# The host lays the chunked weights out so that each 2 MB chunk is 16 KB in a row per partition

## The reference, cut to what matters

```python
sh1, sc1, gt1, sh2, sc2, gt2 = adaln(c, ada_w[l], ada_b[l])       # ada_w: 1024 x 6144
...
x_mix, _, _ = token_mixer(hx @ w_in[l], lbs[l], s_f, s_b, *mix_args)   # w_in: 1024 x 6144
...
mixed = jax.nn.sigmoid(g_a) * (y_a @ w_pa) + jax.nn.sigmoid(g_b) * (y_b @ w_pb)
return mixed @ w_o
...
mod_x = silu_c @ ada_w[layer] + ada_b[layer]                       # second block, two layers
lat = project_in(h, w_in)                                          # w_in: 1024 x 3616
...
def squared_relu_mlp(h, w1, w2):                                   # 1024 x 4096, 4096 x 1024
    return jnp.square(jax.nn.relu(h @ w1)) @ w2
```

## Time and profile before

| | |
|---|---|
| runs | 2148.82, 2149.39, 2142.51 us; median 2148.82 |
| span of the profiled execution | 2142.0 us |
| TensorE busy / weight load | 2005.6 us (94%) / 1431.7 us (67%) |
| DVE, ACT, POOL busy | 34%, 28%, 18% |
| DMA packets | 120207, 428.28 MB |
| mean granted TensorE clock | 0.964 of full speed |

### The profile page before, as it was taken

How to read it: one execution, slowest core, us unless ns; L and a number is a source line. 1 busy time by engine, 2 the same in 40 slices (tenths; PEclk the granted TensorE clock), 3 DMA queues, 4 the chain that set the end, 5 groups by cost and what they waited for, 6 DMA issues and landing times.

```text
span 2142.0 us, 27488 instructions
## 1 busy us (share of the span) xinstructions
PE 2005.6 (94%) x11518; PEld 1431.7 (67%) x11518; DVE 724.0 (34%) x1201; ACT 594.7 (28%) x921; POOL 385.9 (18%) x183
## 2 busy tenths in 40 slices
PE   7799989999999999998999798999999899889998
PEld 2567787775444444446887646777777678579998
DVE  1523154323222222226343614222222535533333
ACT  2413112022222222223113414222332311534443
POOL 2400000000000000005003012333343010414653
PEclk9899978989999999999999899999999999998999
DMA  9268914447999999982224003344334232413450
GB/s 358 96 244 295 369 51 160 160 158 305 425 428 419 426 421 427 423 358 105 100 79 150 1 30 138 138 143 171 137 137 140 78 106 94 157 52 145 158 187 29
DMA packets 120207, 428.28 MB, mean 200 GB/s; under 512 B 5690, under 2 KB 23141, under 8 KB 107456
## 3 DMA queue, kind: packets, MB, share of 16 engines
q1 hardware_dynamic: 118016, 416.56, 50.5%
q0 software_dynamic: 2112, 10.57, 1.4%
HBM read 426.07 MB, written 1.05 MB: 199 GB/s over the span
## 4 chain that ended last, share of the span: by engine, by line
PE 70%; PEld 5%; DVE 4%; issue 3%; ACT 3%; POOL 2%; PEldq 0%; DVEq 0%; ACTq 0%
PE bank L505 68%; PEld bank L505 5%; PE bank L520 1%; DVE H L1805 0%; DVE X L2344 0%; POOL arena L1723 0%; POOL arena L1722 0%; DVE arena L2288 0%; POOL arena L1727 0%; PEldq L494 0%; POOL arena L1725 0%; DVE H_low L1812 0%; POOL arena L1728 0%; DVE H L2260 0%; DVE ring_low L2158 0%
## 5 line engine op out<-in xcount | busy, mean ns | idle before, releaser
L505 PE MATMUL bank<-arena_r 128*128 128x512 f32 (+1 forms) x1920 | 560.7, 357 | 40.3 <-DVE H_low L1812 20.8
L505 PE MATMUL bank<-arena_r,ring_low 128*128 128x512 f32 (+2 forms) x1792 | 567.0, 349 | 20.5 <-DVE H_low L1812 17.5
L505 PEld LDWEIGHTS bank<-arena_r 128*128 128x128 f32 x1920 | 342.9, 192 | 138.9 <-issue 56.0
L505 PEld LDWEIGHTS bank<-arena_r,ring_low 128*128 128x128 f32 (+1 forms) x1792 | 333.5, 191 | 67.5 <-issue 21.8
L505 PE MATMUL bank<-arena 128*128 128x64 bf16 (+9 forms) x2684 | 329.3, 291 | 24.7 <-DMA arena<-in_hy_filt_w 11.9
L505 PEld LDWEIGHTS bank<-arena 128*128 128x128 bf16 (+4 forms) x2684 | 210.5, 141 | 128.1 <-issue 90.9
L505 PE MATMUL bank<-ring,arena 128*64 128x512 f32 x1024 | 278.2, 595 | 1.1 <-ACT arena L1423 0.7
L2344 DVE SCALAR_TENSOR_TENSOR X<-bank,mod,X 128x256 f32<-128x256 f32 x216 | 96.4, 481 | 394.0 <-PE bank L505 394.0
L505 PE MATMUL bank<-H_low,arena_r 128*128 128x512 f32 (+1 forms) x608 | 208.0, 342 | 0.0
L1749 POOL TENSOR_TENSOR ring_low<-ring,arena_r 128x2048 fp32r<-128x2048 f32 x32 | 146.6, 4603 | 118.5 <-ACT arena_r L1611 118.5
L1271 ACT ACTIVATE arena<-bank 128x512 f32<-128x512 f32 (+2 forms) x106 | 52.4, 496 | 413.5 <-PE bank L505 413.2
(11 more groups left out here) (263 smaller groups left out, 1908.0 us busy)
## 6 DMA issues: line engine op xcount, KB each, us to landing
ring<-in_moe_w_gate SPq DMA_DIRECT2D x32, 2048.0 KB, 13.7
ring<-in_w_mlp SPq DMA_DIRECT2D x32, 2048.0 KB, 8.3
ring<-in_w_in SPq DMA_DIRECT2D x26, 2048.0 KB, 8.8
ring<-in_ada_w SPq DMA_DIRECT2D x24, 2048.0 KB, 11.8
ring<-in_moe_w_up SPq DMA_DIRECT2D x17, 2048.0 KB, 9.2
H<-in_moe_w_down SPq DMA_DIRECT2D x16, 2048.0 KB, 16.1
arena<-in_moe_w_up SPq DMA_DIRECT2D x15, 2048.0 KB, 9.5
ring<-in_moe_w_down SPq DMA_DIRECT2D x15, 2048.0 KB, 16.3
```

Of the source, the lines that this page charges most:

```text
L505: ins = nc.tensor.matmul(o, l, r, start=start, stop=stop, skip_group_check=True)
```

## The change

The host cuts each of the matrices into the chunks that the kernel loads and writes every chunk as [128 partitions, k, n], so that the 16 KB of one partition follow each other. The kernel then loads a whole chunk as it stands. Sizes, order, semaphores, buffers and all compute instructions stay. For the chunks of 384 columns of `ada_w_2[1]` a partition has 12 KB in a row, for the 32 columns of the ranks 1 KB.

```diff
+def by_columns(w, n=512):
+    return np.ascontiguousarray(w.reshape(*w.shape[:-2], -1, P, w.shape[-1] // n, n).swapaxes(-4, -2))
+
+def by_rows(w, k=4):
+    return np.ascontiguousarray(w.reshape(*w.shape[:-2], -1, k, P, w.shape[-1]).swapaxes(-3, -2))
...
-        def cols(w, a, n):
-            return w[:, bass.ds(a, n)].rearrange("(k p) n -> p k n", p=P)
-
-        def rows(w, a, n):
-            return w[bass.ds(a, n), :].rearrange("(k p) n -> p k n", p=P)
-
...
-                load(n, cols(T["ada_w"], n * 512, 512), as_cols(n))
+                load(n, T["ada_w"][n], as_cols(n))
             for j in range(12):
                 n = win(j)
-                load(n, cols(T["w_in"], WIN_ORDER[j] * 512, 512), as_cols(n))
+                load(n, T["w_in"][WIN_ORDER[j]], as_cols(n))
...
-            load(MERGE, rows(T["w_proj_a"], 0, 512), as_rows(MERGE))
-            load(MERGE + 1, rows(T["w_proj_b"], 0, 512), as_rows(MERGE + 1))
+            load(MERGE, T["w_proj_a"], as_rows(MERGE))
+            load(MERGE + 1, T["w_proj_b"], as_rows(MERGE + 1))
...
-                    load(first + 2 * j, cols(T["w_in_2"][l], j * 512, 512), as_cols(first + 2 * j))
+                    load(first + 2 * j, T["w_in_2"][l][j], as_cols(first + 2 * j))
...
-                        load(n, cols(T["w_mlp1_2"][l], (i * 2 + h) * 512, 512), as_cols(n), i * per)
+                        load(n, T["w_mlp1_2"][l][i * 2 + h], as_cols(n), i * per)
...
-                        src = T["w_mlp2_2"][l].rearrange("(j k p) n -> j p k n", p=P, k=4)[i * 2 + h]
-                        load(n, src, as_rows(n), i * per)
+                        load(n, T["w_mlp2_2"][l][i * 2 + h], as_rows(n), i * per)
```

More of the change, by code:

```diff
@@ L281, in _ @@
             for n in range(RING):
-                load(n, cols(T["ada_w"], n * 512, 512), as_cols(n))
+                load(n, T["ada_w"][n], as_cols(n))
             for j in range(12):
                 n = win(j)
-                load(n, cols(T["w_in"], WIN_ORDER[j] * 512, 512), as_cols(n))
+                load(n, T["w_in"][WIN_ORDER[j]], as_cols(n))
                 for i in BEHIND[j] if j < 8 else [8 + j]:
                     n += 1
-                    src = cols(T["ada_w"], (4 + i) * 512, 512) if i < 8 else cols(T["ada_w_2"][0], (i - 8) * 512, 512)
+                    src = T["ada_w"][4 + i] if i < 8 else T["ada_w_2"][i - 8]
                     load(n, src, as_cols(n))
-            load(MERGE, rows(T["w_proj_a"], 0, 512), as_rows(MERGE))
-            load(MERGE + 1, rows(T["w_proj_b"], 0, 512), as_rows(MERGE + 1))
+            load(MERGE, T["w_proj_a"], as_rows(MERGE))
+            load(MERGE + 1, T["w_proj_b"], as_rows(MERGE + 1))
             for j in range(2):
                 n = MERGE + 2 + j
-                load(n, cols(T["w_out"], j * 512, 512), as_cols(n))
+                load(n, T["w_out"][j], as_cols(n))
             def expert(c, name, e, turns=None):
@@ L338, in _ @@
                 for j in range(7):
-                    load(first + 2 * j, cols(T["w_in_2"][l], j * 512, 512), as_cols(first + 2 * j))
-                load(first + 14, cols(T["w_in_2"][l], 7 * 512, 2 * RANK), as_cols(first + 14, 2 * RANK))
+                    load(first + 2 * j, T["w_in_2"][l][j], as_cols(first + 2 * j))
+                load(first + 14, T["w_rank_2"][l], as_cols(first + 14, 2 * RANK))
                 for j in range(2):
-                    load(first + 16 + j, cols(T["w_out_2"][l], j * 512, 512), as_cols(first + 16 + j))
+                    load(first + 16 + j, T["w_out_2"][l][j], as_cols(first + 16 + j))
                 with sp.Fori(0, 4) as i:
@@ L350, in _ @@
                             for a in range(2):
-                                load(n, cols(T["ada_w_2"][1], (i * 4 + h * 2 + a) * ADA_COLS, ADA_COLS), as_cols(n, ADA_COLS), i * per)
+                                load(n, T["ada_w_3"][i * 4 + h * 2 + a], as_cols(n, ADA_COLS), i * per)
                                 n += 1
-                        src = T["w_mlp2_2"][l].rearrange("(j k p) n -> j p k n", p=P, k=4)[i * 2 + h]
-                        load(n, src, as_rows(n), i * per)
+                        load(n, T["w_mlp2_2"][l][i * 2 + h], as_rows(n), i * per)
                         n += 1
@@ L2394 @@
         arrays[name] = np.ascontiguousarray(I[name][0].T)
-    for name in ("ada_w", "w_in", "w_proj_a", "w_proj_b", "w_out", "hy_filt_w1", "hy_filt_w2", "hy_filt_w3"):
+    for name in ("hy_filt_w1", "hy_filt_w2", "hy_filt_w3"):
         arrays[name] = I[name][0]
+    for name in ("ada_w", "w_in", "w_out"):
+        arrays[name] = by_columns(I[name][0])
+    for name in ("w_proj_a", "w_proj_b"):
+        arrays[name] = by_rows(I[name][0])[0]
     for name in ("moe_w_gate", "moe_w_up", "moe_w_down"):
@@ L2399 @@
         arrays[name] = a.reshape(NX, *a.shape[3:])
-    for name in ("ada_w_2", "w_in_2", "w_out_2", "w_mlp1_2", "w_mlp2_2"):
-        arrays[name] = I[name]
+    arrays["ada_w_2"] = by_columns(I["ada_w_2"][0])
+    arrays["ada_w_3"] = by_columns(I["ada_w_2"][1], 384)
+    arrays["w_in_2"] = by_columns(I["w_in_2"][:, :, 0:3584])
+    arrays["w_rank_2"] = by_columns(I["w_in_2"][:, :, 3584:], 2 * RANK)[:, 0]
+    arrays["w_out_2"] = by_columns(I["w_out_2"])
+    arrays["w_mlp1_2"] = by_columns(I["w_mlp1_2"])
+    arrays["w_mlp2_2"] = by_rows(I["w_mlp2_2"])
     arrays["wr"] = np.concatenate([I["moe_router_g_w"][0], I["moe_router_e_w"][0].transpose(1, 0, 2).reshape(D, NX)], axis=1)
```

## The result

The changed kernel is slower: 2159.72 us median of four runs (2155.59 to 2161.98) against 2148.43 us (2142.51 to 2149.39, four runs). The medians differ by 11.3 us. The ratio is 1.0061 (95% interval 1.0041 to 1.008), that is 13 us, with 9 to 17 us as its interval. The forecast was +8 us.

What follows compares the result with a forecast made beforehand. PE was taken to bound the kernel, with loads mattering only in the first 125 us. Start +10 us (16 less 6.0), then -2, gave +8 on the median: 2156.8 us, range 2139 to 2162.

Steps and rivals of the forecast that it cites:

- What bounds the kernel: Whole program: PE sets the pace; after some 130 us faster loads are hidden, so the first 125 us decide everything.
- Turns by piece: DMA engines alternate between q1 and POOL's queue by piece, whatever its size; a q1 turn costs POOL's loads 0.62 us, not 0.09.
- The filter tables: POOL's first loads, which PE's first matmul needs: 20 turns beside q1 bring them at 21 us instead of 11.89.
- `ctx`: The input POOL loads after `x` and `pos`: lands at 39.5 us, 14.5 us later, held up by q1's 16 KB pieces.
- The sum beside POOL: DVE's two-operand sum at line 1857, held by up to one POOL split instruction: 0 to 3.4 us, taken as 1.5.
- D: Delay of PE's sums of squares in the start: 16 us, bounds 13 and 18.5; it also moves the end of `spectrum(1)`.
- The gift of 6.0 us: DVE's `norm` runs free ahead of POOL's second split, leaving 11 instructions instead of 26: 6.0 us less.
- After the start: Chunk 9 landing earlier, -1.0 us, and PE's own load waits of 1.5 us shrinking, -1; remaining loads 0.
- the likeliest case: Start loses more than later loads regain: +4 to +12 us around +8, chance 0.55.
- The rival of fair sharing: 16 KB pieces don't hold up POOL's queue as a whole, `ctx` no later: -8 to -10, about 2140 us; chance 0.23.
- The rival of the small delay: Chunk 4 issued only after `ctx`, or filter tables in other turns: delay 8 or 9, +0.5, near 2149 us; chance 0.16.
- the third rival: Loads no quicker, as 2 KB pieces are not their limit; only turns change: around 2149 to 2158 us; chance 0.06.

## Why the prediction held, and where its sizes were off

- **What bounds the kernel** was read rightly. From 130 to 990 us the changed kernel stays 10.6 to 13.0 us behind the kernel before, matmul by matmul, though q1's loads are quicker: no later load was ahead of PE, but for 0.2 us at one place.
- **Turns by piece** is shown, by the counts of 178 to 182 with their 0.9 us for a pair, and by the three sizes of piece.
- **The filter tables** were put at 21 us and came at 21.74; chunk 4's issue at 26.7, it was 26.22; its split at 36, it was 37.39.
- **`ctx`** was put at 39.5 and came at 41.28, over the upper end of 40.1. The mis-sized term is above all the turn beside q1, put at 0.62 + 0.14 = 0.76 us for a pair. Chunk 3, issued at 2.1, landed 27.3 us later, at 29.4 and not by 26, and a pair took some 0.9 us. POOL's pieces alone were put at 0.165 us and take 7 x 16 / 628 = 0.178; over the 44 turns that were counted without q1 that is only 0.6 us.
- **The sum beside POOL** was put at 1.5 us more, at most 3.4; it was 4.1 (6.48 against 2.36). Both of its instructions were held, not one.
- **D**, the delay of PE's sums of squares, was put at 16 us, with bounds of 13 and 18.5. It was 18.7 (45.65 against 26.94), just outside. The end of `spectrum(1)` was to move by all of D and moved by 17.5 (80.15 against 62.66): PE's matmuls of chunk 3 took 1.9 instead of 3.6 us. That is the granted clock of PE, which the prediction had left out: 0.54 there in the kernel before, 1.00 in the changed one (length, busy time of PE, PEld, DVE, ACT and POOL, granted clock, DMA share, GB/s).

```profile
50.30:54.00 3.70, 3.62 (x17) 0.64 (x16) 0.49 (x2) 0.01 (x1) 3.62 (x2) 0.54 1.05 387
...
69.50:71.40 1.90, 1.90 (x17) 0.40 (x16) 0.47 (x2) 0.00 (x0) 0.00 (x0) 1.00 1.03 440
```

- **The gift of 6.0 us** was 6.7: norm ends at 98.8 against 88.05, 10.8 us later, not 17.5.
- **What was not in the sum** is PE's clock once more. PE is 12.6 us behind at the end of its first projection's first half, 1.8 more than norm. Its last matmuls there follow a wait of 5.80 us, and the granted clock is then at the lower of its two levels, 1.2 GHz, for much of the stretch; ten matmuls take 0.63 us or more each instead of 0.39:

```profile
93.00:101.00 8.00, 4.78 (x12) 3.77 (x13) 6.25 (x13) 2.61 (x6) 2.09 (x1) 0.57 0.01 2
```

In the kernel before the wait was longer (13.84 us), but it lay ahead of these matmuls. Their slow ones ran while DVE still made the later blocks, and cost nothing.
- **After the start** 2 us were to come back. The distance does fall by 2, from 12.6 to 10.6 us by 205 us, but not by the terms of the sum. Chunk 9's wait fell from 5.14 to 4.51 us, by 0.6 and not 1.0. PE's own 1.5 us of waits for loads are gone from the list, but the distance falls by only 0.2 at the place where PE had waited. The other 1.2 us are the clock behind chunk 9's wait: in both kernels PE's matmuls there start at the lower level, but in the changed one it rises after seven matmuls and not after thirteen. Between 206 and 307 us the distance grows to 12.5 again, without a new wait of PE; this is the clock too, which stays at the lower level 3.4 us longer. The same stretches of the kernel before and of the changed one, in pairs:

```profile
122.00:129.00 7.00, 5.80 (x14) 4.56 (x15) 1.15 (x1) 0.00 (x0) 0.00 (x0) 0.51 1.05 386
134.00:141.00 7.00, 5.76 (x19) 4.69 (x20) 1.19 (x1) 0.00 (x0) 0.00 (x0) 0.76 1.02 438
...
268.00:298.00 30.00, 27.83 (x136) 24.86 (x136) 16.53 (x29) 5.07 (x8) 0.00 (x0) 0.77 0.10 30
278.00:308.00 30.00, 28.84 (x133) 25.80 (x133) 16.97 (x30) 2.96 (x6) 0.00 (x0) 0.72 0.01 2
```

The timeline of chunk 9's split in the changed kernel and of PE behind it, for the earlier trace rows:

```profile
128.43 2.29 DVE L1871 CAST arena_r<-ring 128x4096 fp32r<-128x4096 f32 x1 [28.89 <-DMA ring<-in_w_in]
...
135.24 0.79 PE L508 MATMUL bank<-arena_r 128*128 128x512 f32 x1 [4.51 <-DVE ring_low L1872]
```

In sum: the start cost 12.6 us instead of 10, of which 1.5 us are D at the end of `spectrum(1)`, 1.8 the clock behind it, and -0.7 the larger gift. Of the 2 us behind it 0.8 came from the loads, and the clock gave and took the rest. How much of that is kept, a difference of medians of 11.3 us with an interval of 9 to 17 cannot tell.

The path through the start was right at each step, and the forecast is 2.9 us off. Some of that is luck: the clock, which the forecast did not count, moved PE by 1 to 2 us four times up to 307 us, twice each way. The chances were less sure than the path. No change had 0.41 and slower by more than 6.4 us 0.36, and it was the latter that came. The range of 2139 to 2162 us and the likeliest case's 2152 to 2161 both hold 2159.72 only near their upper ends.

The rival of fair sharing falls with the counts. The rival of the small delay supposed that chunk 4 goes out only after `ctx` is in, which takes away chunk 4's 5 us and the hold of the sum. In the changed kernel it went out at 26.22, before `ctx`. The run with chunk 4 behind `ctx` made the condition true: `ctx` landed 5.2 us earlier and the sum ran free. But D was 11.1 us there (38.04 against 26.94), not 8 or 9, and the kernel was still 5.5 us slower than the kernel before, not 0.5. Chunks 0 to 3 alone are enough for a loss. The loads are quicker, so the third rival is out as well: for the same bytes q1's packets took 47.9% of 2156.1 us instead of 50.5% of 2142.0, 49 us less in 108 changed loads, or 0.45 us for each, where 0.5 was forecast.

What stays open is why PE's clock rises earlier in one kernel and later in the other. It also makes the way behind 990 us in the profiled execution, where the distance goes from 13.0 up to 18.8 and back to 14.1. From 990 to 1800 us the kernel before is at the lower level for 33 us and the changed kernel, over the same matmuls, for 50, by the clock records of the two traces; from there to the end it is 33 against 21. PE's idle time differs by at most 0.5 us in either part. In the variants, too, the distance comes and goes there in steps of 1 to 2 us; none of the runs was made to find out what moves the clock.

## What to carry to other kernels

Before transfers on one queue get longer pieces, look who shares the DMA engines with them. If the engines take turns by piece, a queue with small pieces and urgent data pays for the other's size, and it pays from the first moment on. A quicker load is worth something only where it is late; where it frees an issuing engine early, ask what the transfers that now start sooner run into. And when an operation of one engine holds another's, moving it behind costs one line: here it was worth 12.5 us on the changed kernel and 15.6 us on the kernel before (0.6 and 0.7%), more than the layout has been seen to win anywhere.

## What the runs showed of the hardware that was not expected

- A recorded packet of POOL's queue is not one piece: the rows of `x`, `pos` and `ctx` are 1 KB in a row, yet 628 packets carried 2.44 MB, 3.9 KB each. SP's queue did not join its 2 KB pieces: 3440 packets for 6.94 MB, 2.0 KB each. So "turn by piece" in the prediction should read "turn by recorded packet", and the sentence ahead of it, that a DMA packet is one piece in a row on both sides, holds for SP's queue only.
- Packets joined in this way run at 349 GB/s with the engines to themselves, against 386 for SP's 2 KB and 424 for its 16 KB pieces.
- SP's issue of four loads took 27.57 us with 2 KB pieces and 2.59 us with 16 KB pieces: with eight times the pieces SP is held much longer. That hold had an effect of its own, as it kept chunk 4 behind `ctx`.
